# DeltaNet's prefix one to three units later between the second projection's units, and three pairs of the triangular solve's steps behind one unit each

## What is computed

```python
proj = x @ p['w_in1']
conv = lax.conv_general_dilated(xc, gdn_conv_w, ...)         # causal, width 4, q, k and v
qc, kc, vc = _split(jax.nn.silu(conv), ...)
qc, kc = _l2norm(qc) * DK_C ** -0.5, _l2norm(kc)
...
gc = jnp.cumsum(g, axis=-1)
A = beta[..., :, None] * jnp.einsum('bhtd,bhsd->bhts', k, k) * dec_strict
rhs = jnp.concatenate([beta[..., None] * v, (beta * jnp.exp(gc))[..., None] * k], -1)
sol = lax.linalg.triangular_solve(A + jnp.eye(c), rhs, left_side=True, lower=True, unit_diagonal=True)
...
qk = jnp.einsum('bhtd,bhsd->bhts', q, k) * dec_incl
```

## Time and profile before

| | |
|---|---|
| time of three runs, us | 1542.83, 1544.57, 1544.66; median 1544.57 |
| the profiled execution, us | 1545.56, of which the span of the trace is 1543.7 |
| busy share of the span | TensorE 92%, VectorE 63%, ScalarE 48%, GpSimd 15% |
| mean granted clock of TensorE | 0.922 of 2.4 GHz |
| second projection in the trace | 526.4 to 699.6 us |

### The profile page before, as it was taken

The page is one execution under the profiler, slowest core; times in us unless marked ns, Lnnn a source line. Parts: engine busy times, 40 slices in busy tenths (PEclk is TensorE's granted clock), DMA queues, the critical chain, the costliest instruction groups (busy, mean ns, idle before and its releaser), DMA issues.

```text
span 1543.7 us, 18458 instructions
## 1 busy us (share of the span) xinstructions
PE 1423.6 (92%) x7933; PEld 1240.2 (80%) x7933; DVE 977.1 (63%) x939; ACT 744.3 (48%) x622; POOL 231.3 (15%) x166
## 2 busy tenths in 40 slices
PE   7999999799999789998989767999999999999994
PEld 6898886799999578996676666788888888888883
DVE  4533366554553657742535556688988889888886
ACT  4434322432332674321313325577766777677771
POOL 0110303000000000001222030000000002366562
PEclk9999997899999988998556958999999999999998
DMA  6422634645424122211132528799999996400002
GB/s 242 155 96 82 230 96 129 210 123 184 147 83 144 45 69 69 87 55 55 26 118 79 199 87 313 275 377 372 374 391 379 374 372 236 164 28 14 15 14 97
DMA packets 80891, 254.81 MB, mean 165 GB/s; under 512 B 11569, under 2 KB 47701, under 8 KB 68009
## 3 DMA queue, kind: packets, MB, share of 16 engines
q1 hardware_dynamic: 66008, 224.53, 40.3%
q0 software_dynamic: 14800, 29.10, 6.1%
HBM read 306.09 MB, written 16.70 MB: 209 GB/s over the span
## 4 chain that ended last, share of the span: by engine, by line
PE 79%; DVE 7%; DMA 6%; ACT 5%; issue 3%; POOL 0%; POOLq 0%; SPq 0%; DVEq 0%; ACTq 0%
PE PS L612 11%; PE PS L614 10%; PE PS L613 10%; PE PS L1271 7%; PE PS L1273 7%; PE PS L1276 7%; DMA u_raw<-in_w_moe 4%; PE PS L592 3%; PE PS L1294 2%; PE PS L1298 2%; PE PS L1295 2%; PE PS L1008 2%; ACT u_hi L1656 1%; PE PS L677 1%; PE PS L739 1%
## 5 line engine op out<-in xcount | busy, mean ns | idle before, releaser
L2509 DVE TENSOR_TENSOR u_lo<-u_raw,u_hi 128x2816 fp32r<-128x2816 f32 x144 | 442.1, 3089 | 106.2 <-ACT u_hi L1656 105.8
L1656 ACT ACTIVATE u_hi<-u_raw 128x2816 fp32r<-128x2816 f32 x144 | 367.5, 2561 | 181.7 <-DMA u_raw<-in_w_moe 115.5
L612 PE MATMUL PS<-x_in_hi,p_hi 128*128 128x304 f32 x480 | 159.9, 333 | 10.6 <-DVE x_in_lo L1898 10.6
L613 PE MATMUL PS<-x_in_lo,p_hi 128*128 128x304 f32 x480 | 149.6, 312 | 0.0
L614 PE MATMUL PS<-x_in_hi,p_lo 128*128 128x304 f32 x480 | 149.6, 312 | 0.0
L1271 PE MATMUL PS<-u_hi,xg_hi 128*128 128x512 f32 x576 | 142.5, 380 | 5.6 <-DVE xg_lo L2588 3.2
L1273 PE MATMUL PS<-u_hi,xg_lo 128*128 128x512 f32 x576 | 141.3, 377 | 0.0
L1276 PE MATMUL PS<-u_lo,xg_hi 128*128 128x512 f32 x576 | 140.1, 375 | 0.0
L612 PE MATMUL PS<-x_out_hi,w_parts 128*128 128x304 f32 x416 | 128.2, 308 | 8.5 <-DVE x_out_lo L1898 8.5
L614 PE MATMUL PS<-x_out_hi,w_parts 128*128 128x304 f32 x416 | 127.3, 306 | 0.0
L613 PE MATMUL PS<-x_out_lo,w_parts 128*128 128x304 f32 x416 | 126.8, 305 | 0.0
(11 more groups left out here) (545 smaller groups left out, 2527.5 us busy)
## 6 DMA issues: line engine op xcount, KB each, us to landing
u_raw<-in_w_moe SPq DMA_DIRECT2D x96, 1408.0 KB, 8.5
p_raw<-in_w_first SPq DMA_DIRECT2D x40, 512.0 KB, 3.5
p_raw<-in_w_second SPq DMA_DIRECT2D x28, 512.0 KB, 3.5
dring<-in_ffn_w_down SPq DMA_DIRECT2D x8, 1408.0 KB, 7.1
wring<-in_ffn_w_gate SPq DMA_DIRECT2D x9, 1024.0 KB, 5.5
wring<-in_ffn_w_up SPq DMA_DIRECT2D x9, 1024.0 KB, 8.5
wring<-in_w_out SPq DMA_DIRECT2D x2, 2048.0 KB, 7.7
o_rows<-zT POOLq DMA_DIRECT2D x6, 512.0 KB, 6.0
```

Source lines behind the costliest of these rows:

```text
L612: mm(out, w[0], x[0], start=start, stop=False)
L613: mm(out, w[0], x[1], start=False, stop=False)
L1656: A(uhi[n % HIS][:], uraw[n % RAW][:], COPY).then_inc(s("u_hi"), 1)
L2509: TT(ulo[n % RAW][:], uraw[n % RAW][:], uhi[n % HIS][:].bitcast(F32), SUB).then_inc(s("u_lo"), 1)
```

## The change

The extra work of the three loops moves to other iterations, in TensorE's, ScalarE's and VectorE's loop alike; nothing is added or removed. On TensorE the gate rows' transposes move from behind unit 2 to behind unit 3, the broadcasts and sums by one unit as well, the key products from behind unit 7 to behind unit 9, the key tokens and the solve's first step as shown, query norms and scores by two units. The solve's steps 0 to 8 stand behind units 12 to 20 (before: 9 to 17), steps 9 to 14 in pairs behind units 21, 22 and 23, and steps 15 to 17 behind units 24 to 26, as before. Value tokens stay behind units 19 and 20. The core of the diff:

```diff
-SOLVE_AT = 9
+SOLVE_IN = {12 + k: [k] for k in range(9)} | {21: [9, 10], 22: [11, 12], 23: [13, 14], 24: [15], 25: [16], 26: [17]}
...
@@ TensorE
-                if n == 2:
+                if n == 3:
                     pe.wait_ge(*at("g_rows", 1))
...
-                if n == 7:
+                if n == 9:
                     pe.wait_ge(*at("g_l2a", 1))
                     pe.wait_ge(*at("g_kb", 1))
...
-                if n == 8:
+                if n == 10:
                     pe.wait_ge(*at("g_bcev", 2))
                     for i in range(2):
                         tokens(4 + i, i, 4).then_inc(s("g_kt"), 1)
-                if n == 9:
+                if n == 12:
                     pe.wait_ge(*at("g_at", 1))
-                if SOLVE_AT <= n < SOLVE_AT + len(SOLVE):
-                    solve(n - SOLVE_AT)
-                if n == 9:
+                for k in SOLVE_IN.get(n, ()):
+                    solve(k)
+                if n == 11:
                     pe.wait_ge(*at("g_tok_d", 1))
                     tokens(4, 2, 4).then_inc(s("g_kt"), 1)
...
@@ ScalarE
-                if n == 2:
+                if n == 3:
                     act.wait_ge(*at("g_gc", 1))
...
-                if n == 5:
+                if n == 6:
                     act.wait_ge(*at("convs", 4))
                     A(sqn, P[:, 4:8, :], SQR).then_inc(s("g_sqn"), 1)
-                if n == 6:
+                if n == 7:
                     act.wait_ge(*at("g_l2pe", 1))
                     A(sqn, bank4(0), LN, bias=EPS).then_inc(s("g_l2a"), 1)
...
@@ VectorE
-                if SOLVE_AT < n:
-                    if n - 1 - SOLVE_AT < len(SOLVE):
-                        solve(n - 1 - SOLVE_AT)
+                for k in SOLVE_IN.get(n - 1, ()):
+                    solve(k)
                 if n + 2 < NU1:
                     unit1_lo(n + 2)
-                if n < 3:
-                    g_rows(n)
-                if n == 3:
+                if n in (0, 1, 3):
+                    g_rows(n - n // 2)
+                if n == 4:
                     dve.wait_ge(*at("g_colpe", 1))
...
-                if n == 7:
+                if n == 8:
                     dve.wait_ge(*at("g_l2r", 1))
                     link(TT(P[:, 4:8, :], P[:, 4:8, :], sqn, MUL))
                     TT(kb, P[:, 4:8, :], kb, MUL).then_inc(s("g_kb"), 1)
-                if n == 8:
+                if n == 10:
                     dve.wait_ge(*at("g_aa", 4))
```

More of the change, by code:

```diff
@@ L1025, in _ @@
                     g_beta_rows([0, 1])
-                if n == 4:
+                if n == 5:
                     pe.wait_ge(*at("g_bcev", 1))
                     g_beta_rows([2, 3])
-                if n == 5:
+                if n == 6:
                     pe.wait_ge(*at("g_sqn", 1))
@@ L1046, in _ @@
                         tokens(4 + i, i, 4).then_inc(s("g_kt"), 1)
-                if n == 9:
+                if n == 12:
                     pe.wait_ge(*at("g_at", 1))
-                if SOLVE_AT <= n < SOLVE_AT + len(SOLVE):
-                    solve(n - SOLVE_AT)
-                if n == 9:
+                for k in SOLVE_IN.get(n, ()):
+                    solve(k)
+                if n == 11:
                     pe.wait_ge(*at("g_tok_d", 1))
                     tokens(4, 2, 4).then_inc(s("g_kt"), 1)
-                if n in (11, 12):
+                if n in (13, 14):
                     pe.wait_ge(*at("g_sqn", 2))
-                    pe.wait_ge(*[at("g_tok_d", 3), at("g_l2a", 2)][n - 11])
+                    pe.wait_ge(*[at("g_tok_d", 3), at("g_l2a", 2)][n - 13])
                     for m in range(2):
-                        last = mm(PS[:, 4 + m, 0:T], ones, sqn[:, 2 * (n - 11) + m, :], start=True, stop=True)
+                        last = mm(PS[:, 4 + m, 0:T], ones, sqn[:, 2 * (n - 13) + m, :], start=True, stop=True)
                     last.then_inc(s("g_l2pe"), 1)
-                if n == 14:
+                if n == 16:
                     pe.wait_ge(*at("g_l2a", 3))
@@ L1063, in _ @@
                     g_scores([0, 1])
-                if n == 15:
+                if n == 17:
                     pe.wait_ge(*at("g_att", 1))
@@ L1576, in _ @@
                         last.then_inc(s("g_dec"), 1)
-                if n == 9:
+                if n == 11:
                     key_tokens(0)
                     key_tokens(1)
-                if n == 10:
+                if n == 12:
                     key_tokens(2)
-                if n == 11:
+                if n == 13:
                     act.wait_ge(*at("convs", 8))
@@ L1585, in _ @@
                     A(sqn, P[:, 0:4, :], SQR).then_inc(s("g_sqn"), 1)
-                if n in (12, 13):
-                    c = n - 12
+                if n in (14, 15):
+                    c = n - 14
                     act.wait_ge(*at("g_l2pe", 2 + c))
                     A(sqn[:, 2 * c:2 * c + 2, :], PS[:, 4:6, 0:T], LN, bias=EPS).then_inc(s("g_l2a"), 1)
-                if n == 13:
+                if n == 15:
                     act.wait_ge(*at("g_l2a", 3))
@@ L2393, in _ @@
                     TT(qe, qe, P[:, 0:4, :], MUL)
-                if n in (15, 16):
-                    g_scores(n - 15)
+                if n in (17, 18):
+                    g_scores(n - 17)
                 if n == 20:
```

## The result

The changed kernel took 1534.49 us in the median (1527.42 to 1540.06, 6 executions) beside 1544.60 of the kernel before (1539.40 to 1546.93, 6): a ratio of 0.9948, interval 0.9925 to 0.9970. Run again beside other executions of before it gave 1536.42 beside 1541.95, 0.9959 (0.9938 to 0.9981). The ratios are those on record with their intervals; the medians alone would give 0.9935 and 0.9964. So it is faster, by some 6 to 8 us by the ratios, more than the 4.7 us forecast. The execution that the profile shows took 1540.06 us, 5.6 above that median; its span is 1538.2.

A forecast was written before the change was run, and what follows sets the result against it. TensorE's chain of waits was taken as the bound, 79% of the time; 0.0 - 1.5 + 0.0 - 2.8 - 0.4 + 0.0 = -4.7 us gave 1540.9 for the profiled execution, 1539.9 as forecast, range 1536.5 to 1544.0.

The forecast's parts named there:

- First stall: TensorE's 5.3 us wait ahead of the gate rows' transposes: VectorE's rows move equally, 3.43 us later, so 0.0.
- Second stall: TensorE's wait ahead of the key products: 3.7 us instead of 5.2, start 5.4 us later with two units more, -1.5.
- Clock behind the second stall: Key products and the unit behind them, 11.24 us: same clock loss of 5.0 us taken, 0.0; bounds -2.2 and +1.7.
- the clock is spared: Rival behind the shorter key-product wait: -2.2 gives 1537.7, no drop at all -5.0 and 1534.9; chance 0.12.
- signs of being wrong: Key-product wait above 4.8, wait over 1 us at L1008 or scores from unit 16, or low clock lasting otherwise than told.
- First steps of the solve: Solve's second step waiting for the split of the first: some 0.4 us of wait left of 3.2, -2.8.
- the unit behind them: Projection unit behind the solve's waiting step: 4.00 us at 0.87 becomes an ordinary 3.5 to 3.6, -0.4.
- The tail: Solve steps 9 to 14 in pairs behind units 21 to 23, 15 to 17 unmoved: no wait, 0.0.
- the pairs choke: Rival in the tail: VectorE's copies late, paired steps wait, 9.9 us on top, 1549.8; chance 0.08.
- the stalls that move along: Rival: engines' pieces move as far as TensorE's in the other two stalls too, nothing gained, 1544.6; chance 0.18.
- The sum: All terms in the second projection together: -4.7 us, giving 1540.9 for the profiled execution, 1539.9 as median.
- the gain should arrive whole: Behind the projection: everything waits for its end in turn, so its gain should reach the kernel's time whole.

The follow-up runs named there:

- Rows early: Changed kernel with the gate rows' last two VectorE operations and their ScalarE exponentials back in iteration 2; ratio 0.9943 to the kernel before.
- second profile: Profile of the changed kernel run once more with no edit; ratio 0.9959 to the kernel before.
- no pairs: Changed kernel with one solve step behind each unit from 12 on, steps 15 to 17 behind the last unit; ratio 1.0000 to the kernel before.
- rows and columns early: Changed kernel with gate rows (VectorE, ScalarE) and VectorE's column copies each one iteration earlier; ratios 0.9917 and 0.9915 to the kernel before in two runs.
- solve alone: Kernel before with only the solve's steps at their new places, the prefix unmoved; ratio 1.0002 to the kernel before.
- keys later: Changed kernel with key products behind unit 10, mask and solve one unit later, steps 6 and 7 paired; ratio 0.9960 to the kernel before.
- early and keys later: Changed kernel with gate rows and column copies an iteration earlier, key products behind unit 10, mask and solve a unit later; ratio 0.9914 to the kernel before.
- and tokens later: Changed kernel with early gate rows and columns, key products behind unit 10, third tile's key tokens behind unit 12; 1526.12 us beside 1543.64, ratio 0.9896.

## Why the prediction was right, point by point

- **First stall, 0.0: right.** TensorE went on 19.1 us after the start of the projection (543.55 less 524.44), 15.6 before (542.08 less 526.44): 3.5 later, with a unit more done. VectorE's timeline of after shows the convolution and the low part that stand ahead of the gate rows:

```profile
539.51 0.17 DVE L2278 COPY arena<-cst 128x24 f32<-128x24 f32 x1
...
541.81 1.22 DVE L1908 TENSOR_TENSOR p_lo<-p_raw,p_hi 128x1024 fp32r<-128x1024 f32 x1
542.95 0.46 DVE L2270 TENSOR_TENSOR stB<-stB 4x304 f32<-4x304 f32 x1
```

From 539.51 to 542.95 are 3.44 us, where 3.43 were told. Behind the stall stand 7.22 us at 0.53 and, in the next unit, 4.84 at 0.70, as taken (7.27 and 4.90). "Rows early" then showed the other half: leave VectorE's rows where they were, and TensorE's unit more is worth 3.4 of wait.

- **Second stall, -1.5: right.** The key products started 55.3 us into the projection, 50.0 before: 5.3 later (5.4 told), with two units more in front. The wait is 3.30 (3.7 told), and 0.10 stand at unit 9 as told: a gain of 1.75. In the second profile they started 56.8 us in, and the waits are the same. ScalarE's timeline of after shows the chain:

```profile
564.05 0.40 ACT L1600 ACTIVATE arena<-PS 128x272 f32<-128x272 f32 x1 [2.23 <-PE PS L614]
...
566.32 1.04 ACT L1365 ACTIVATE p_hi<-p_raw 128x1024 fp32r<-128x1024 f32 x1
...
569.88 1.28 ACT L1570 ACT_TABLE_LOAD   x1
571.18 1.22 ACT L1570 ACTIVATE dring<-dring 128x1216 f32<-128x1216 f32 x1
...
574.48 1.04 ACT L1365 ACTIVATE p_hi<-p_raw 128x1024 fp32r<-128x1024 f32 x1
```

The chain begins 2.27 us behind the eviction (2.3 told) and its two high parts are 8.16 apart (8.25 told). The load of 1.28 from 569.88 is followed by the exponential at 571.18, 0.02 behind it. The drain of 1380 ns that the Trainium skill (ScalarE: Activation LUTs, What ACT_TABLE_LOAD costs) adds to a load isn't there either; by it this wait would be some 4.7, an estimate (3.30 and 1.38).

- **Clock behind the second stall, 0.0: right in one trace, 1.5 too small in the other.** Key products and the unit behind them took 11.24 before, 11.19 and 9.78 in the two profiles of the change. The rival that the clock is spared came in with 1.5 of its 2.2 once, and the unit behind the first stall, taken as it was, cost 1.4 more than before in the other profile (6.29 for 4.90). So one of the prediction's own signs of being wrong, a low clock that lasts otherwise than told, came in with either profile. The two are of one kernel with the same waits, so what differs between them isn't the change's doing. The length of the wait doesn't tell the cost either: from the first key product to the end of the unit behind, the four other profiles with a wait of 3.30 ("no pairs", "rows early", both of "rows and columns early") took 11.1, 9.8, 10.8 and 10.9, and "solve alone", with 5.2, took 10.5.

- **First steps of the solve, -2.8, and the unit behind them, -0.4: right.** 5.45 became 2.87 (-2.6), with a wait of 0.35 (0.4 told), and 4.00 became 3.56 (-0.4). VectorE's third tile starts its last releasing operation at 604.15 and is ready at 604.50, where TensorE goes on at 604.56. Counted from unit 0 that is 1.5 us earlier than told, and in the second profile it is 1.5 later; the wait is the same in both, since both engines' times shift together:

```profile
604.15 0.35 DVE L2340 TENSOR_TENSOR mix<-PS,zT 48x192 f32<-48x192 f32 x1
```

"Solve alone" shows that this term hangs on the prefix: with it unmoved 1.4 of the 1.7 of wait come back elsewhere.

- **The tail, 0.0: right.** From 609.50 to 691.68 TensorE is busy for 82.11 of 82.18 us at 1.00. The first pair in the chain of after, two steps of 1.78 as told:

```profile
654.80 3.57 PE PS L1008 x32
```

The rival that the pairs choke is refuted; so is that of the stalls that move along, for the second stall and the solve, though it is what holds for the first.

- **The sum.** In the projection -4.7 was told; the two profiles give -6.05 and -3.18, a mean of -4.6. With the second stall at -1.75, the solve and its unit at -2.6 and -0.4, and the clock at -1.46 (first) or at -0.05 and +1.4 (second), they add to -6.2 and -3.4. The stalls came as told; that the mean meets the forecast is luck, since the clock put one profile 1.35 us beyond it and the other 1.5 short.

- **What was missing: the step "the gain should arrive whole".** It took the 187 us to the router as unchanged; they are 3.05 and 2.6 shorter in the two profiles, of which 1.2 are lost again between the router and the mixture of experts. So the time came out below the forecast (1534.49 and 1536.42 for 1539.9, at and under the low end of the range). 2.6 of the 3.05 are L739's 16 matmuls (6.95 before, 4.36 after). The waits there are the same; the clock behind them is not. I had read the drop behind the wait at L739 as what such a wait brings. The Trainium skill (TensorE: Matmul & The Clock Gate, What's actually happening) says that the point at which the clock rises varies from run to run of the same kernel; the two profiles of the change, with 9.78 and 11.19 us for the same work behind the same wait, agree.

What decides the clock on the way to the router stays open. Three kernels with nothing altered in that code need 182.9 (keys later), 187.3 (early and keys later) and 191.6 (solve alone); the two pairs of profiles of one kernel agree (184.3 and 184.7; 184.3 and 184.4). That it hangs on when TensorE gets there is a guess that no run here tested. It decides two verdicts: "solve alone" and "no pairs" lose there (4.3 us against before, and 9.0 against the change) what they gain in the projection.

## What to carry to other kernels

Where every engine's order is written out, a step gains from a later place only as far as TensorE gets more units in front of it than the engine that feeds it gets work: shift the consumer alone, and look for the next step that waits behind the same feeder (rows, then columns; keys, then tokens). Price a removed wait with the clock behind it, but as a bound: the same wait was followed by 9.78 and by 11.19 us of the same work. Where a change is worth a few us, sum the stretches of the trace up to a common point, and take two profiles of a kernel before reading a clock stretch as the change's doing.

## What the runs showed of the hardware that was not expected

A wait doesn't always bring the lower clock at once. In "and tokens later" TensorE worked for 6.46 us without a hole at 1.00 behind a wait of 1.95, and only then came 6.82 us at 0.50:

```profile
535.92:542.38 6.46, 6.45 (x44) 5.61 (x45) 6.14 (x14) 4.42 (x12) 1.32 (x2) 1.00 0.28 91
542.38:549.20 6.82, 6.82 (x23) 5.66 (x22) 4.46 (x11) 3.74 (x5) 0.00 (x0) 0.50 0.10 42
...
571.25:574.65 3.40, 3.40 (x27) 2.70 (x25) 3.26 (x7) 3.37 (x11) 1.28 (x2) 1.00 0.44 154
```

The fall came with the broadcasts (L1024, L983), whose factor has four rows. In the first profile of the change, too, a fall came there: TensorE was back at 1.00 when it began the broadcasts, worked through them without a hole, and began the unit behind them at 0.50.

```profile
550.77:553.00 2.23, 2.23 (x9) 1.58 (x9) 0.28 (x1) 1.81 (x4) 0.00 (x0) 1.00 0.42 125
...
554.34:557.04 2.70, 2.70 (x11) 2.70 (x11) 0.79 (x1) 2.57 (x3) 0.00 (x0) 0.50 0.00 0
```

So the low clock of that unit, which the prediction books to the first stall (0.71 before), need not be the stall's. Whether the wait, the broadcasts or both bring it, these runs don't tell apart.

The last row of "and tokens later" is the key products with no wait ahead of them: 3.40 us at 1.00, against 4.77 in the first profile of the change and 5.89 in the second, for the same 24 matmuls behind a wait of 3.30. So a wait of 3.3 cost up to 2.5 us more than its length in these matmuls alone.
